# Two mixture-of-experts layers on one core: token counts in five products, two picks moved behind the first expert's rows, the last shared down product in column groups

## What is computed

```python
scores = jax.nn.sigmoid(x2d @ router)                  # 272 x 64
...                                                    # group-limited choice of 8 experts a token, gate weights
order = jnp.argsort(e_flat)                            # token rows by expert
...
def expert_block(args):
    tok, e, gt = args
    y = swiglu(x2d[tok], w_gate[e], w_up[e], w_down[e])
    return y * gt[:, None]
...
return swiglu(x2d, sh_gate, sh_up, sh_down) + routed   # shared expert + sum over a token's 8 experts
```

## Time and profile before

| | |
|---|---|
| median of 3 runs | 1621.53 us (1621.11 to 1623.51) |
| the profiled execution's own time | 1621.35 us |
| its span in the profile | 1619.6 us |
| TensorE busy | 1449.4 us, 89% of the span |
| VectorE, ScalarE, GpSimd busy | 38%, 20%, 20% |
| read from memory over the span | 332 GB/s |
| expert stage of layer 0, of layer 1 | 371 to 886 us, 1065 to 1580 us |

### The profile page before, as it was taken

How to read it: one execution, slowest core, us unless ns; L and a number is a source line. 1 busy time by engine, 2 the same in 40 slices (tenths; PEclk the granted TensorE clock), 3 DMA queues, 4 the chain that set the end, 5 groups by cost and what they waited for, 6 DMA issues and landing times.

```text
span 1619.6 us, 33331 instructions
## 1 busy us (share of the span) xinstructions
PE 1449.4 (89%) x12804; PEld 937.7 (58%) x12804; DVE 614.1 (38%) x1580; ACT 318.4 (20%) x743; POOL 327.4 (20%) x404
## 2 busy tenths in 40 slices
PE   6989988799999998888886699999999998888884
PEld 4777878647556655555553267575566655555541
DVE  5352343654333333333322704453333333223326
ACT  2531333111111111111111016211111111111110
POOL 6012000011222222222222030022222222222210
PEclk9999989799999999999999799999999999999998
DMA  6340002496999999999997995469999999999986
GB/s 203 113 130 1 3 4 81 163 360 255 394 413 413 414 415 416 415 415 415 415 415 301 374 321 183 159 232 395 412 412 414 415 415 415 416 415 416 415 339 254
DMA packets 139878, 508.42 MB, mean 314 GB/s; under 512 B 29273, under 2 KB 58273, under 8 KB 104188
## 3 DMA queue, kind: packets, MB, share of 16 engines
q1 hardware_dynamic: 103312, 456.49, 70.9%
q0 software_dynamic: 22288, 41.89, 7.3%
q10 hardware_dynamic: 14172, 8.54, 1.9%
HBM read 501.38 MB, written 36.90 MB: 332 GB/s over the span
## 4 chain that ended last, share of the span: by engine, by line
PE 55%; SPq 27%; DMA 8%; DVE 6%; issue 3%; ACT 1%; POOL 0%; POOLq 0%; DVEq 0%
SPq L836 27%; PE ps L784 13%; PE ps L802 7%; PE ps L1466 6%; DMA arena<-in_moe_w_up 5%; PE ps L1596 3%; PE ps L765 3%; PE ps L772 2%; PE ps L1019 2%; PE ps L1898 2%; PE ps L2000 2%; DMA ring<-in_moe_w_up 2%; PE ps L1029 1%; PE ps L791 1%; DMA arena<-routed 1%
## 5 line engine op out<-in xcount | busy, mean ns | idle before, releaser
L784 PE MATMUL ps<-arena 128*64 128x256 f32 x2752 | 314.4, 381 | 54.2 <-DMA arena<-in_moe_w_up 42.7
L784 PEld LDWEIGHTS ps<-arena 128*64 128x64 f32 x2752 | 211.1, 137 | 187.1 <-issue 117.0
L777 DVE COPY arena<-ps 128x512 f32<-128x512 f32 x128 | 88.5, 692 | 448.9 <-PE ps L772 448.9
L821 POOL DMA_INDIRECT arena<-hrows,arena x128 | 130.3, 1018 | 548.4 <-DVE arena L817 532.7
L784 PE MATMUL ps<-ring,arena 128*64 128x256 f32 x1344 | 153.5, 381 | 23.6 <-DMA ring<-in_moe_w_up 22.0
L826 POOL DMA_INDIRECT routed<-arena x128 | 117.0, 914 | 246.6 <-DVE arena L952 226.7
L802 PE MATMUL ps<-arena 128*64 128x512 f32 x688 | 166.6, 605 | 0.0
L952 DVE TENSOR_SCALAR arena<-ps,arena 64x512 f32<-64x512 f32 x128 | 95.1, 743 | 167.8 <-PE ps L802 167.8
L784 PEld LDWEIGHTS ps<-ring,arena 128*64 128x64 f32 x1344 | 99.8, 137 | 90.9 <-issue 37.2
L906 ACT COPY arena<-ps 128x256 f32<-128x256 f32 x128 | 47.6, 372 | 495.7 <-PE ps L784 495.7
L916 ACT ACTIVATE arena<-ps,arena 64x512 f32<-64x512 f32 x128 | 87.5, 683 | 208.2 <-PE ps L802 208.2
(11 more groups left out here) (360 smaller groups left out, 1533.0 us busy)
## 6 DMA issues: line engine op xcount, KB each, us to landing
arena<-in_moe_w_down SPq DMA_DIRECT2D x86, 1024.0 KB, 24.2
arena<-in_moe_w_gate SPq DMA_DIRECT2D x86, 1024.0 KB, 24.5
arena<-in_moe_w_up SPq DMA_DIRECT2D x86, 1024.0 KB, 24.4
ring<-in_moe_w_gate SPq DMA_DIRECT2D x42, 1024.0 KB, 24.5
ring<-in_moe_w_up SPq DMA_DIRECT2D x42, 1024.0 KB, 24.3
ring<-in_moe_w_down SPq DMA_DIRECT2D x42, 1024.0 KB, 24.1
arena<-routed SPq DMA_DIRECT2D x16, 1024.0 KB, 14.6
ring<-in_attn_w_qkv SPq DMA_DIRECT2D x6, 1024.0 KB, 16.4
```

Of the source, the lines that this page charges most:

```text
L777: return nc.vector.tensor_copy(xgT.rearrange("p (r j) m -> p j r m", r=2), ps[:, bU, :].rearrange("p (j r m) -> p j r m", j=4, r=2))
L784: mm = nc.tensor.matmul(dst[SLOTS * j:SLOTS * j + SLOTS, 0:FF], xgT[:, k, :], slots[pair[j]][:, FF * k:FF * k + FF], start=(k == 0), stop= ...
L821: return nc.gpsimd.indirect_dma_start(out=dst, out_offset=None, in_=hrows_d[l], in_offset=bass.IndirectOffsetOnAxis(ap=index, axis=0), bou ...
```

## The change

Three places. The counts of `pos` are made by five products: `allones` of a tile is multiplied with the mask repeated over all later tiles at once (192, then 128 columns), and the triangle with tiles 1 and 2 together. The picks of experts 1 and 2 leave the shared products: pick 1 stands behind the transposes of expert 0, pick 2 behind gate and up of expert 0; VectorE's instructions follow, so index 1 comes after the copy of expert 0's rows and index 2 inside expert 0's turn. The shared down products are five units at turns 1 to 5: the tile of 16 tokens takes one unit, four column groups of 256 columns, and VectorE adds it in four pieces.

```diff
-                        + [..., ("su0", 1), ("su1", 1), ("sd", 6)])
+                        + [..., ("su0", 1), ("su1", 1), ("sd", 5)])
...
-                            ("kr", 1), ("dest", 3), ("posm", 1), ("sm0", 1), ("max", 1), ("maxi", 1), ("sm1", 1),
-                            ("sd", 6)]) for l in range(2)]
+                            ("kr", 1), ("dest", 3), ("posm", 1), ("sm0", 1), ("sm1", 1), ("max", 1), ("maxi", 1),
+                            ("sd", 5)]) for l in range(2)]
...
                 mm_gate_up(ps[:, bG, :], (s0, s1)).then_inc(L.gu, 1)
+                if early(e, 0):
+                    pe_pick(pe, L, (0, 2))
             if this and after:
                 pe_turn_x(pe, L, l, plus(e, 1))
...
                 dve_mark(dve, L, plus(e, 3))
+            if this and early(e, 0):
+                dve_index(dve, L, (0, 2))
             if this and ahead(e, 1):
                 dve_copy_xt(dve, L, plus(e, 1))
...
-        DOWN_TURNS = (1, 2, 3, 5, 6, 7)
+        DOWN_TURNS = (1, 2, 3, 4, 5)
...
             for j in range(2):
+                for q in range(4 if u == 4 else 0):
+                    m = nc.tensor.matmul(ps[32 * q:32 * q + n, bS[0], 0:256], shm[:, j, r0:r0 + n],
+                                         shared_w[2][:, D * j + 256 * q:][:, 0:256], start=(j == 0), stop=(j == 1))
+                if u == 4:
+                    continue
...
             pe_pick(pe, L, (0, 0))
             mm_shared(pe, l, "su0", range(2, KC))
-            pe_pick(pe, L, (0, 1))
-            mm_shared(pe, l, "su1", range(KC // 2))
-            pe_pick(pe, L, (0, 2))
-            mm_shared(pe, l, "su1", range(KC // 2, KC))
+            mm_shared(pe, l, "su1", range(KC))
             pe.wait_ge(*moe_act[l].at("sg1"))
             pe_turn_x(pe, L, l, (0, 0))
+            pe_pick(pe, L, (0, 1))
...
+            if u == 4:
+                for q in range(4):
+                    cs = slice(256 * q, 256 * q + 256)
+                    add = nc.vector.scalar_tensor_tensor(out=h[0:n, 2, cs], in0=h[0:n, 2, cs], scalar=ALPHA,
+                                                         in1=ps[32 * q:32 * q + n, bS[0], 0:256], op0=ALU.mult, op1=ALU.add)
+                add.then_inc(*moe_dve[l].step("sd", u))
+                return
...
             dve_index(dve, L, (0, 0))
             dve_mark(dve, L, (0, 2))
+            dve_shared(dve, l, 0)
+            dve_copy_xt(dve, L, (0, 0))
             dve_index(dve, L, (0, 1))
-            dve_shared(dve, l, 0)
-            dve_index(dve, L, (0, 2))
-            dve_copy_xt(dve, L, (0, 0))
+            dve_shared(dve, l, 1)
             nc.vector.tensor_reduce(most, ps[:, bC, NT * E:NT * E + E], AX.X, ALU.max).then_inc(*moe_dve[l].step("max"))
...
-            dve_shared(dve, l, 1)
...
-                for t in range(NT + 1):
-                    for t2 in range(min(t + 1, NT)):
-                        k2 = TILES[t2][1]
-                        m = mm_(ps[:, bC, E * t:E * t + E], (before if t2 == t else allones)[0:k2, :], sel[0:k2, t2, :],
-                                start=(t2 == 0), stop=(t2 == min(t, NT - 1)))
+                few_rows = TILES[-1][1]
+                for t2 in range(NT - 1):
+                    mm_(ps[:, bC, E * (t2 + 1):NT * E + E].rearrange("p (t e) -> p t e", e=E), allones[:, :],
+                        sel[:, t2, :].unsqueeze(1).to_broadcast([P, NT - t2, E]), start=(t2 == 0), stop=False)
+                mm_(ps[:, bC, NT * E:NT * E + E], allones[0:few_rows, :], sel[0:few_rows, NT - 1, :], start=False,
+                    stop=False)
+                mm_(ps[:, bC, 0:E], before[:, :], sel[:, 0, :], start=False, stop=False)
+                m = mm_(ps[:, bC, E:NT * E], before[:, :], sel[:, 1:NT, :].rearrange("p t e -> p (t e)"), start=False,
+                        stop=True)
```

More of the change, by code:

```diff
@@ L281, in hybrid_trunk @@
         moe_pe = [Steps(sem(f"route_pe{l}"), [(f"hT{t}", 1 if t == 2 else 2) for t in H_ORDER[l]]
-                        + [("lg", 1), ("sT", 1), ("sg0", 1), ("sg1", 1), ("pos", 1), ("su0", 1), ("su1", 1), ("sd", 6)])
+                        + [("lg", 1), ("sT", 1), ("sg0", 1), ("sg1", 1), ("pos", 1), ("su0", 1), ("su1", 1), ("sd", 5)])
                   for l in range(2)]
```

## The result

The changed kernel is slower: 1631.52 us, median of 13 runs (1626.62 to 1638.81), against 1623.14 us for the kernel before, also 13 runs (1616.34 to 1630.02, and one of 6039.69 us, without which the median would be 1622.34). The ratio is 1.0054 with a 95% interval of 1.0035 to 1.0073, thus about 8.8 us. The profiled execution of the changed kernel took 1626.62 us, the lowest of its 13; that is 5.3 us over the profiled execution of before.

What follows compares the result with a forecast made beforehand. The prediction took the expert weight stream to bound the kernel: 5.7 us lost per layer, net 2.3 after earlier losses and the earlier start, 4.6 for both layers on 1621.35, giving 1626.0 us; range 1619.5 to 1631.5.

Steps and rivals of the forecast that it cites:

- before 395: Layer 0, second freed pair of weight loads: issue before 395 us would prove the prediction wrong; forecast near 396.7.
- The second gather starts at 10.3: Gather of expert 1, layer 0: starts at 384.9 us, beside the weight stream, and takes 6.7 us to land.
- the early gather: Rival: expert 1's gather still lands early, in 3.7 us; not slower, 1619 to 1621.5 us; chance 0.19.
- The wait of 3.5: TensorE, after pick 2, waits 3.5 us for the gather of expert 1.
- The second pair at 22.1: Second freed pair of weight loads, layer 0: issued at 396.7 us instead of 393.98.
- The gap of 3.3 in the stream: Weight stream, layer 0: dry at 395.5 us, new data at 398.8, so 3.3 us lost.
- The four turns of 0.6: Experts 1 to 5 follow each other in 9 us against the stream's 8.4: 2.4 us lost per layer.
- by the same rule: Kernel before: stream loss per layer counted by 9 us turns against 8.4, 0.6 each; given as 1.5 us.
- The last down unit 0.9 to 1.8: New last shared down unit on TensorE, turn 5: 0.9 us taken, 1.8 at most, then 0.3 more lost.
- long gather, clock kept: The forecast case: expert 1's gather lands late, TensorE keeps full clock; 1626.0 us, chance 0.50.
- the clock falls in the new wait: Rival: the wait ahead of expert 1 halves TensorE's clock, 4.2 us more in both layers, 1630.2 us; chance 0.20.
- The term for the stream: Weight stream, each layer: 5.7 us lost, less earlier losses and a 1.3 us earlier start, net 2.3.

Runs made afterwards that it cites:

- e2: The kernel before with only the moved picks, their indices and VectorE's order: 1625.72 us, ratio 1.0022.
- e6: The changed kernel with pick 1 and its index back ahead of su1, pick 2 behind the transposes of expert 0: 1621.50 us, ratio 0.9986.
- e10: The changed kernel with picks, indices and VectorE's order as before, so only counts and down units changed: 1624.45 us, ratio 1.0001.
- e8: The changed kernel with SyncE loading the last two slots only when the gather of expert 1 has landed: 1629.05 us, one run.
- e3: The kernel before with only the five shared down units at turns 1 to 5: 1623.37 us, ratio 0.9985.
- e5: The changed kernel with half of su0 instead of a quarter ahead of the first pick: 1629.65 us, ratio 1.0041.
- e4: The changed kernel with three unread products on TensorE behind pick 2, filling the wait ahead of expert 1: 1627.68 us, ratio 1.0025.
- e9: The changed kernel with half of su0 ahead of the first pick and three unread products ahead of expert 1's transposes: 1629.46 us, ratio 1.0023.
- e1: The kernel before with only the five products for the counts of pos: 1624.26 us, ratio 0.9987.
- e7: The changed kernel with pick 1 ahead of su1, pick 2 behind expert 0's transposes, half of su0 first, down units at turns 1, 2, 3, 5, 6: 1618.66 us, ratio 0.9966.

## Why the prediction was right or wrong

**Right: the direction, and the chain up to TensorE's wait and from the late pair on.** The time is bound by the weight stream; the counts bring nothing, since VectorE's chain and not the counts set `posm`; the picks that leave the shared products bring the slots' loads forward; the second gather then starts beside the stream, lands late, TensorE waits, the second pair is late and the stream has a gap from 392 to 395 us. Each of these is in the trace, in both layers, and e2, e6 and e10 show that it hangs on the picks.

**Point by point**, in us after the first pick where nothing else is said. In this execution the first pick comes 3.6 us earlier than in the one before, so the prediction's clock times have to be moved: the pair issued at 393.70 us stands where 397.3 would stand before, and does not break the sign "before 395".

- Slots 1.3 earlier than before: measured 1.7 (9.28 to 7.57).
- The second gather starts at 10.3 (384.9 less 374.58): measured 9.85. Its landing 6.7: measured 5.8 and 5.5, below all 61 of the earlier trace rows and above the first three. For the early gather I had weighed what the Trainium skill, "DMA: Bandwidth & Descriptors", section "Queues, rings and completion order", states: the DMA engines take turns between queues packet by packet. The rows agree in the steady state, where a gather lands in 6.3 to 8.2 us and the weight load of the earlier trace rows takes 24.49. In this place the runs can't tell a share from a place behind the loads ahead of it: two slots, 2.1 MB, take 5.1 us at 415 GB/s, and the landing was 5.8 beside the stream against 3.3 without it (e8). For the rival, which needed under 5, it was too late.
- The wait of 3.5: measured 2.41 and 2.16, from the shorter landing.
- The clock: see below.
- The second pair at 22.1 (396.7 less 374.58): measured 22.70 and 22.42. Right by two errors that cancel, a wait 1.1 to 1.3 us too long and 1.7 us of half clock (5.36 less 3.67) left out.
- The gap of 3.3 in the stream, from 20.9 to 24.2 after the first pick (395.5 and 398.8 less 374.58): it came from 21 to 24 (392 to 395 less 371.00), and the stretches from 388.5 to 397 us lose 0.6 + 2.7 + 0.4 = 3.7 us against 415 GB/s. The four turns of 0.6, 2.4 in all: the 36 us from 400 at 375 GB/s lose 3.5. (The 1.5 lost before "by the same rule" is not worked out in the prediction: turns 1 to 3 at 0.6 would be 1.8, the row says 2.7.)
- The last down unit 0.9 to 1.8: measured 1.06; units at turns 1 to 5 by themselves cost nothing (e3). That a turn of 9 us costs more once the stock is gone fits this, but no run shows it by itself.

**The step that failed** is the clock. I chose the case "long gather, clock kept", at 0.50, over "the clock falls in the new wait", 0.20. From the earlier trace rows I had a wait of 4.38 us that ended at half clock and one of 3.14 us that kept full clock, and put a wait of 3.5 us on the safe side. The waits were shorter than either, 2.2 to 2.4 us in the changed kernel, and the clock fell behind them or in their last us in every layer that had one ahead of expert 1 (both layers of the changed kernel, of e2 and of e5). The length of a wait does not order these cases. Even the earlier trace rows could have told: a mean clock of 0.70 over the 4.38 us means that it fell within the wait, and the stretches of that trace, the kernel before, show that it fell 1.7 us after the wait began (columns as above):

```profile
107.00:108.70 1.70, 0.00 (x0) 0.00 (x0) 1.70 (x5) 0.00 (x0) 0.10 (x1) 1.00 0.84 296
108.70:111.38 2.68, 0.00 (x0) 0.00 (x0) 2.68 (x8) 0.00 (x0) 0.00 (x0) 0.50 0.04 9
```

And the rest between the two expert stages, 3.14 us in the earlier trace rows with the clock kept, was 3.15 us in the changed kernel, and there the clock fell behind it for 3.4 us (first row the rest, second what follows 0.5 us later):

```profile
907.08:910.23 3.15, 0.00 (x1) 0.00 (x0) 2.90 (x3) 0.00 (x0) 0.00 (x0) 1.00 1.02 427
910.76:914.17 3.41, 3.41 (x5) 1.35 (x4) 3.30 (x6) 0.29 (x1) 0.00 (x0) 0.50 1.01 420
```

In layer 1 of e8 a wait of 2.24 us kept the clock. What decides between a fall and none stays open here. The Trainium skill, "TensorE: Matmul & The Clock Gate", section "HAM oscillation — how this bites in real kernels", describes waits for DMA between stretches of matmuls that put the array back to half clock; the waits it describes are longer, some 3 to 5 us. The traces agree with its direction in the six waits ahead of expert 1, all but one of them shorter than that, and not in e8's wait of 2.24 us.

**What it did to the sum.** The term for the stream was 5.7 us lost per layer, net 2.3, in all 4.6. Measured: 7.7 and 6.5 lost, stages 3.65 and 2.54 longer, in all 6.2. The fall cost gate and up of expert 1 1.7 us, a term that the sum had at nothing; the shorter landing gave most of that back, so that the second pair came nearly when forecast. The terms that were also too small are the turns behind the gap, 2.4 against 3.5, and the gap, 3.3 against 3.7; the earlier start, 1.3 against 1.7, was too small the other way. The rival's own time, 1630.2, is the one nearest to the measured median, but in part by luck: its added time, 8.8 us, is further from the 6.2 us of the stages than the 4.6 us of the forecast.

How the 6.2 us part between late gather and clock is not settled. Without a fall, the layer with a late gather was 1.7 us over before in e4's layer 1, and e9's two layers were 2.6 over, where the stream starts 0.9 us earlier in each (6.65 against 7.57 after the first pick). In layer 1 alone the clock's part is 0.8 of 2.5 us (504.10 less 503.27).

**The rest of the miss.** The measured median is 5.5 us over the forecast. 1.6 of it are the stages (6.2 less 4.6). 1.8 are the base: I summed on the profiled 1621.35 us, and the kernel before had a median of 1623.14 over 13 runs. The other 2.1 us are open: the fall behind the first pick could give them (five layers in twelve, some 2 us each as e1 and e6 have it between their two layers, two layers an execution: 1.7 us), but e1 and e10, which have that wait, show no loss in their medians, and the intervals are wider than 2 us.

## What to carry to other kernels

A small step that is moved out of the way takes its whole chain with it: here three tiny products, an index and a gather. The gather started 4.1 us later (9.85 against 5.74 us after the first pick, layer 0) and took 5.8 us instead of 3.15, because it now ran beside the stream that the move had brought forward. Ask of each transfer that is moved what runs beside it then, and start what the next stage waits for ahead of the bulk loads (e7). A wait that a cheap edit opens on TensorE can cost more behind it than in it: price it with its clock, and compare stage times as well as medians when the run around the stage scatters more than the effect.

## What was not expected of the hardware

- TensorE's clock fell to 0.50 behind a wait of 0.86 or 0.87 us, in five of twelve layers with the same instructions around it, for 3.4 us each time. Waits of 2.16 to 3.83 us ahead of expert 1 came with a fall in all six layers that had them, while a wait of 2.24 us ahead of expert 2 did not (e8, layer 1). The rest of 3.15 us between the expert stages had a fall behind it in the changed kernel and none in the kernel before.
- The same gather took 3.3 us beside almost no other load (e8) and 5.4 to 5.8 us beside a stream of 400 GB/s that had only just begun, once 7.21 us (e5, layer 1).
- Three products whose result nobody reads, 2.84 us of them in a wait of some 2.2 us, kept the clock there in all four layers that had them (e4, e9).
